# Hgrn mixer of a two-block denoiser on one core: heads in pieces inside projection blocks, and the output product taken apart by heads

## The reference, cut to what matters

```python
def hgrn2_mixer(h_lat, h_ctx, w_in, ...):            # 512 latent and 256 context tokens
    qc, vc, zfc, zbc, gc = _hgrn_inputs(h_ctx, w_in)    # h @ w_in, 1024 x 5120, in 8 heads of 128
    ql, vl, zfl, zbl, gl = _hgrn_inputs(h_lat, w_in)
    ... _gate(z, lb): log_f = log(lb + (1-lb) sigmoid(z)), k = (1-lb) sigmoid(-z), both directions
    ... _gla_scan in chunks of 64 tokens, forward and backward:
        cum = cumsum(log_f); scores = (q exp(cum-ref)) (k exp(ref-cum))^T, masked by a triangle
        S_next = exp(last) S + k^T v; o = scores v + (q exp(cum)) S
    y_lat = _hgrn_readout(o_lf + _rev(o_lb), gl, gnorm, w_out)

def _hgrn_readout(o, g, gnorm, w_out):
    o = o * rsqrt(mean(o * o, -1) + EPS) * gnorm        # per head
    y = o * silu(g)
    return y @ w_out                                     # 1024 x 1024, the sum goes over all 8 heads

x_lat = x_lat + g1 * y_lat
```

## Time and profile before

| | us |
|---|---|
| median of three runs (lowest, highest) | 3496.42 (3491.14, 3500.28) |
| the profiled execution | 3493.21 |
| its span | 3491.5 |
| mean granted TensorE clock | 0.947 |
| TensorE busy (products) | 3158.1, 90% |
| VectorE busy | 1861.7, 53% |
| ScalarE busy | 1387.5, 40% |
| the mixer with its output product, from the first block to the norm sum behind it | about 90 to 736 us of the span |

### The profile page before, as it was taken

One profiled execution on the slowest core, in us unless ns is written; L12 is line 12 of the kernel. 1 busy time (PEld: TensorE's weight loads), 2 busy tenths in 40 slices (PEclk: granted clock), 3 DMA queues, 4 the chain that ended last, 5 costly groups with the idle time before them and its releaser, 6 DMA issues.

```text
span 3491.5 us, 44906 instructions
## 1 busy us (share of the span) xinstructions
PE 3158.1 (90%) x16582; PEld 2570.7 (74%) x16582; DVE 1861.7 (53%) x2627; ACT 1387.5 (40%) x1905; POOL 116.1 (3%) x121
## 2 busy tenths in 40 slices
PE   5988888578996999899888999999998999889997
PEld 4777777467875888766776888878887778678886
DVE  6554555367985443678536534563446333454435
ACT  4445544446874222456314322342224332342222
POOL 0000000000000000043100000000000000000000
PEclk8999989698998999999998999999999999999998
DMA  4311211138992222221001222222222222123322
GB/s 170 127 55 57 70 54 54 37 120 337 390 359 83 96 96 96 85 71 61 23 2 61 96 96 96 102 88 97 93 95 97 73 73 90 50 71 103 101 97 73
DMA packets 98049, 357.66 MB, mean 102 GB/s; under 512 B 11008, under 2 KB 11392, under 8 KB 97536
## 3 DMA queue, kind: packets, MB, share of 16 engines
q1 hardware_dynamic: 92448, 334.54, 27.5%
q0 software_dynamic: 4176, 15.24, 1.2%
q10 hardware_dynamic: 1296, 6.11, 0.5%
HBM read 344.29 MB, written 11.56 MB: 102 GB/s over the span
## 4 chain that ended last, share of the span: by engine, by line
PE 78%; DVE 9%; ACT 7%; issue 4%; DMA 1%; POOL 0%; ACTq 0%; DVEq 0%; POOLq 0%
PE bank L281 20%; PE bank L282 19%; PE bank L283 19%; PE bank L1622 1%; PE bank L1624 1%; PE bank L1623 1%; PE gbank L920 1%; ACT whi L259 1%; PE bank L2603 1%; ACT L352 1%; DVE cum L1066 1%; PE gbank L902 1%; PE gbank L937 1%; PE bank L1651 1%; PE bank L1650 1%
## 5 line engine op out<-in xcount | busy, mean ns | idle before, releaser
L281 PE MATMUL bank<-h_hi_buf,whi 128*128 128x512 f32 x2320 | 929.5, 401 | 53.7 <-DVE h_lo_buf L450 33.9
L282 PE MATMUL bank<-h_lo_buf,whi 128*128 128x512 f32 x2320 | 912.6, 393 | 0.0
L283 PE MATMUL bank<-h_hi_buf,wlo 128*128 128x512 f32 x2320 | 911.0, 393 | 0.0
L259 ACT ACTIVATE whi<-raw 128x1024 fp32r<-128x1024 f32 x466 | 477.3, 1049 | 456.5 <-PE bank L283 402.3
L272 DVE TENSOR_TENSOR wlo<-raw,whi 128x1024 fp32r<-128x1024 f32 x444 | 533.4, 1221 | 138.6 <-ACT whi L259 71.8
L281 PEld LDWEIGHTS bank<-h_hi_buf,whi 128*128 128x128 f32 x2320 | 442.4, 191 | 167.5 <-DVE h_lo_buf L450 42.7
L282 PEld LDWEIGHTS bank<-h_lo_buf,whi 128*128 128x128 f32 x2320 | 442.2, 191 | 95.2 <-issue 5.3
L283 PEld LDWEIGHTS bank<-h_hi_buf,wlo 128*128 128x128 f32 x2320 | 441.4, 190 | 93.9
L281 PE MATMUL bank<-a_hi_buf,whi 128*128 128x512 f32 x960 | 377.1, 393 | 25.0 <-DVE a_lo_buf L3184 9.6
L282 PE MATMUL bank<-a_lo_buf,whi 128*128 128x512 f32 x960 | 375.7, 391 | 0.0
L283 PE MATMUL bank<-a_hi_buf,wlo 128*128 128x512 f32 x960 | 375.6, 391 | 0.0
(11 more groups left out here) (512 smaller groups left out, 3803.3 us busy)
## 6 DMA issues: line engine op xcount, KB each, us to landing
raw<-in_w SPq DMA_DIRECT2D x634, 512.0 KB, 3.4
x<-in_x ACTq DMA_DIRECT2D x2, 2048.0 KB, 10.8
sorted_rows<-zrow POOLq DMA_DIRECT2D x7, 514.0 KB, 8.4
xrow<-sorted_rows POOLq DMA_DIRECT2D x7, 514.0 KB, 7.5
sorted_y<-ysb POOLq DMA_DIRECT2D x7, 512.0 KB, 7.4
out<-x SPq DMA_DIRECT2D x8, 256.0 KB, 2.0
xc<-in_xc ACTq DMA_DIRECT2D x1, 1024.0 KB, 8.7
waup<-in_waup ACTq DMA_DIRECT2D x1, 256.0 KB, 5.2
```

The costliest lines, as they stand in the source:

```text
L259: act.activation(k.whi[:, g.slot, :], k.raw[:, g.slot, :], ACT.Copy).then_inc(k.split_hi, 1)
L281: pe.matmul(out, w_hi, hi, start=(t == 0), stop=False)
L282: pe.matmul(out, w_hi, lo, start=False, stop=False)
L283: return pe.matmul(out, w_lo, hi, start=False, stop=(t == tiles - 1))
```

## The change

**Three stages of the pipeline in place of two.** In iteration h the blocks of head h are multiplied, head e = h - 1 goes through its mixer, and the readout of head f = h - 2 is finished (squares, norm, gate, high and low part of y). Iterations 0 to 2 are unrolled, 3 to 7 are the loop.

**TensorE's pieces lie inside blocks.** `pe_block` already takes a call per tile (`ready`); it is now used to issue the pieces between the tiles of a block: the norm sum of f in block 0 at tile 4, v's transposes behind block 0, the two keys' in QB at tiles 4 and 7, the scores and the first state lot in VB at tiles 2 and 6, the second and third state lot in GB at tiles 0 and 4, the output behind GB.

**State products over 64 rows.** The products take rows 0 to 63 or 64 to 127 of `ktok` and of the one full `vtok`; `v_half` is gone with its four copies and its memset. The lots are three in place of six, and hold both directions; the bank goes by the half of rows (`c % 2`), no longer by the direction.

**The output product by heads.** A tile is (o, t): output rows o, head t. `PARTIAL` lists the 56 tiles of the first seven heads; the weights are packed in that order on the host (`partial_blocks`), the eight tiles of the last head in a block of their own. `pe_tail` multiplies the 56 (`fill(n)` takes the next n tiles of the list) between the pieces of head 7's mixer, into the four banks and `cbank`. VectorE adds each finished partial sum into x (`dve_partial`, eight times); `HgrnOutput` then multiplies the last head's eight tiles and VectorE adds these too. x is asked for when the last projection block is done. The memset of `ssq` is gone.

```diff
+EARLY = [(o, t) for o in range(RING + 1) for t in range(HEADS - 2)]
+PARTIAL = EARLY + [(o, HEADS - 2) for o in range(RING + 1)] + [(o, t) for o in range(RING + 1, DC) for t in range(HEADS - 1)]
+
+
+def partial_bank(k, o):
+
+    return k.bank[o] if o < RING else k.cbank if o == RING else k.bank[o - RING - 1]
...
+        def at_first(t):
...
+            if f is not None and t == 4:
+                self.pe_norm(k, q, f)
+
+        def at_query(t):
+            if e is not None and t in (4, 7):
+                self.pe_keys(k, e, 0 if t == 4 else 1)
+
+        def at_value(t):
+            if e is not None and t == 2:
+                self.pe_scores(k, e)
+            if e is not None and t == 6:
+                self.pe_states(k, e, 0)
+
+        def at_gate(t):
+            if e is not None and t in (0, 4):
+                self.pe_states(k, e, 1 if t == 0 else 2)
...
+        pe_block(k, g + ZB, DC, lat, more=(con, h.count(3, 1)))
+        pe_block(k, g + QB, DC, lat, ready=at_query)
+        pe_block(k, g + VB, DC, lat, more=(con, h.count(3, 2)), ready=at_value)
+        pe_block(k, g + GB, DC, lat, ready=at_gate)
         if e is not None:
+            self.pe_output(k, e)
...
+        for i, j in enumerate(range(4 * lot, min(4 * lot + 4, STEPS))):
+            for d in range(2):
                 c = CHAIN[d][j]
+                half = slice(CH * (c % 2), CH * (c % 2) + CH)
+                last = pe.matmul(k.gbank[c % 2][:, i * P:(i + 1) * P], k.ktok[half, d, c // 2, :], k.vtok[half, c // 2, :],
+                                 start=True, stop=True)
+        last.then_inc(k.gla_full, 1)
...
+    def pe_tail(self, k, q, e, f):
+
...
+        fill(4)
+        self.pe_norm(k, q, f)
+        self.pe_values(k, e)
+        fill(len(EARLY) - 4)
+        for d in range(2):
+            self.pe_keys(k, e, d)
+        fill(2)
+        self.pe_scores(k, e)
+        fill(3)
+        for lot, behind in enumerate((3, 4, 4)):
+            self.pe_states(k, e, lot)
+            fill(behind)
+        self.pe_output(k, e)
+        fill(4)
+        self.pe_norm(k, q, e)
+        fill(len(PARTIAL) - n)
+
+    def pe_partial(self, k, g, n):
+
         pe = k.nc.tensor
+        o, t = PARTIAL[n]
+        b = n // DC
+        out = partial_bank(k, o)[:, :]
+        wait(pe, k.split_lo, g + b + 1)
+        wait(pe, k.y_parts, t + 1)
+        if t == 0 and o < RING:
+            wait(pe, k.bank_free, g)
+        elif t == 0:
+            wait(pe, k.cbank_free if o == RING else k.partial_taken, 3 * HEADS if o == RING else o - RING)
+        w = slice(n % DC * P, (n % DC + 1) * P)
+        w_hi, w_lo = k.whi[:, (g + b) % RING, w], k.wlo[:, (g + b) % RING, w]
+        pe.matmul(out, w_hi, k.a_hi_buf[:, t, :], start=(t == 0), stop=False)
+        pe.matmul(out, w_hi, k.a_lo_buf[:, t, :], start=False, stop=False)
+        last = pe.matmul(out, w_lo, k.a_hi_buf[:, t, :], start=False, stop=(t == HEADS - 2))
+        if n % DC == DC - 1:
+            last.then_inc(k.block_done, 1)
+        elif t == HEADS - 2:
+            last.then_inc(k.out_full, 1)
...
+    def act_iteration(self, k, q, h, e, f):
+        g = h.n.times(HEAD_BLOCKS) + q.g
         def split(b):
+            act_split(k, g + b + LEAD)
         split(0)
+        if f is not None:
+            self.act_square_of(k, f)
         split(1)
         if e is not None:
+            self.act_sigmoids(k, q, e, f)
         split(2)
         if e is not None:
+            self.act_decays(k, e)
+        if f is not None:
+            self.act_norm_log(k, q, f)
         if e is not None:
+            self.act_turned(k, e, 0, k.vtok)
         split(3)
+        if f is not None:
+            self.act_norm_exp(k, q, f)
         if e is not None:
+            self.act_exponents(k, e)
         split(4)
         split(5)
         split(6)
         if e is not None:
+            self.act_turned(k, e, 2, k.ktok[:, 0])
+        if f is not None:
+            self.act_high(k, f)
+        if e is not None:
+            self.act_turned(k, e, 4, k.ktok[:, 1])
         split(7)
         if e is not None:
+            self.act_states(k, e, range(3, STEPS))
...
+        g = q.g + self.blocks
+        act.wait_ge(k.block_done, g)
+        act.dma_start(k.x[:, :, :], k.xT).then_inc(k.x_loaded, 16)
+        self.act_square_of(k, f)
+        self.act_sigmoids(k, q, e, f)
+        act_split(k, At(g + LEAD))
+        self.act_decays(k, e)
+        self.act_norm_log(k, q, f)
+        self.act_turned(k, e, 0, k.vtok)
+        act_split(k, At(g + LEAD + 1))
+        self.act_norm_exp(k, q, f)
+        self.act_exponents(k, e)
+        act_split(k, At(g + LEAD + 2))
+        self.act_high(k, f)
+        self.act_turned(k, e, 2, k.ktok[:, 0])
+        self.act_turned(k, e, 4, k.ktok[:, 1])
+        act_split(k, At(g + LEAD + 3))
+        self.act_states(k, e, range(3, 7))
+        act_split(k, At(g + LEAD + 4))
+        self.act_states(k, e, range(7, STEPS))
+        self.act_square_of(k, e)
+        act_split(k, At(g + LEAD + 5))
+        self.act_norm_log(k, q, e)
+        self.act_norm_exp(k, q, e)
+        self.act_high(k, e)
...
+        split(0)
+        if f is not None:
+            self.dve_gated(k, f)
+        split(1)
         if e is not None:
         take(0, k.z_st[:, 0, :], context=True)
+        if e is not None:
+            self.dve_silus(k, e)
         split(2)
         if e is not None:
+            for d in range(2):
+                self.dve_scan(k, e, d)
+        wait(dve, k.block_done, g + MOD_BLOCKS + 1)
+        dve_mod(k, k.bank[1][:, 0:MOD_BLOCKS * P], MOD_BLOCKS, h.n.times(MOD_BLOCKS) + 2 * DC, 0,
+                h.n + 2 * (2 * DC // RING), g + MOD_BLOCKS + 1, MOD_BLOCKS)
         split(3)
         if e is not None:
+            self.dve_keys(k, e)
         take(ZB, k.z_st[:, 1, :], context=True)
         split(4)
+        if f is not None:
+            self.dve_scaled(k, q, f)
         split(5)
         if e is not None:
+            wait(dve, k.qq_done, e.count(2, 2))
+        take(QB, k.q_st[:, :])
+        split(6)
+        if f is not None:
+            self.dve_low(k, f, e)
+        if e is not None:
+            if f is None:
+                wait(dve, k.gla_full, e.count(G_HEAD, N_TOK + N_SC))
             for d in range(2):
                 dve.copy_predicated(k.pt[:, d, :, :], k.pt_mask[:, d, :, :],
                                     k.gbank[d][:, :].rearrange("p (j t) -> p j t", t=P)).then_inc(k.pt_ready, 1)
+            self.dve_chain(k, e, 0)
         take(VB, k.v_st[:, :], context=True)
         if e is not None:
+            self.dve_chain(k, e, 1)
+            self.dve_chain(k, e, 2)
             wait(dve, k.silg_done, e.count(1, 1))
         take(GB, k.g_st[:, :])
         split(7)
         if e is not None:
+            self.dve_taken(k, e)
...
+        g = q.g + self.blocks
+        self.dve_gated(k, f)
+        self.dve_residual_gates(k)
+        self.dve_silus(k, e)
+        dve_split(k, At(g + LEAD))
+        for d in range(2):
+            self.dve_scan(k, e, d)
+        dve_split(k, At(g + LEAD + 1))
+        self.dve_keys(k, e)
+        wait(dve, k.qq_done, e.count(2, 2))
+        self.dve_scaled(k, q, f)
+        dve_split(k, At(g + LEAD + 2))
+        self.dve_low(k, f)
+        dve.wait_ge(k.x_loaded, 48)
+        for o in range(2):
+            self.dve_partial(k, g, o)
+        self.dve_masked(k, e)
+        self.dve_chain(k, e, 0)
+        self.dve_partial(k, g, 2)
+        self.dve_chain(k, e, 1)
+        dve_split(k, At(g + LEAD + 3))
+        self.dve_chain(k, e, 2)
+        for o in range(3, RING + 1):
+            self.dve_partial(k, g, o)
+        dve_split(k, At(g + LEAD + 4))
+        self.dve_taken(k, e)
+        self.dve_partial(k, g, RING + 1)
+        self.dve_gated(k, e)
+        self.dve_partial(k, g, RING + 2)
+        self.dve_scaled(k, q, e)
+        self.dve_low(k, e)
+        dve_split(k, At(g + LEAD + 5))
...
         pe = k.nc.tensor
+        t = HEADS - 1
+        wait(pe, k.split_lo, q.g + DC)
         pe.wait_ge(k.y_parts, HEADS)
+        for o in range(DC):
+            if o < RING:
+                wait(pe, k.partial_taken, o + RING + 2 if o < RING - 1 else RING)
+            else:
+                wait(pe, k.bank_free, q.g + o - RING + 1)
+            out, slot, w = k.bank[o % RING][:, :], (q.g + DC - 1) % RING, slice(o * P, (o + 1) * P)
+            pe.matmul(out, k.whi[:, slot, w], k.a_hi_buf[:, t, :], start=True, stop=False)
+            pe.matmul(out, k.whi[:, slot, w], k.a_lo_buf[:, t, :], start=False, stop=False)
+            last = pe.matmul(out, k.wlo[:, slot, w], k.a_hi_buf[:, t, :], start=False, stop=True)
+            last.then_inc(k.out_full if o < DC - 1 else k.block_done, 1)
 
     def act(self, k, q):
         act = k.nc.scalar
         k.sq, k.h32 = k.sq0, k.h320
+        for c in range(DC):
+            act_square(k, k.x[:, c, :], At(c + q.sq), lambda act: wait(act, k.bank_free, q.g + c + 1))
```

(16 more changed lines are left out.)

479 lines of the change are left out of this document (241 added, 238 removed).

## The result

The changed kernel takes **3343.3 us** (median of 4 runs, 3340.4 to 3345.7) against 3493.8 for the kernel before beside it (4 runs, 3488.2 to 3500.3): 0.9568 of its time, 95% interval 0.9549 to 0.9588. The profiled execution took 3340.36 us, its span is 3338.6.

A forecast was written before the change was run, and what follows sets the result against it. TensorE, with 78% of the critical chain, was taken as the bound, idling inside mixer lumps. Gains 86.4 (six periods), 6 (first) and 41.5 (last head), 134 us, took 3493.2 to 3359; plus 3.2 for the median, 3362; range 3344 to 3392.

The forecast's parts named there:

- The period without the state products: Loop head on TensorE: 54.9 us of full-clock work in all, counting 22 state products at 0.225 each.
- The 64-row products: State products in the loop: still 22 and not overlapping, with 0.2 us a lot for switching, 0.6 a head.
- the overlap rival: State products: consecutive ones in opposite row halves run together, saving 2.5 us a head, 3344; chance 0.05.
- Waits and hand-overs left in the loop: TensorE in a loop head: waits of 9.5 us shrink to about 0.5, plus 0.3 for hand-overs.
- The walk: Loop head followed engine by engine from the preceding output; tightest at the q block, its split 0.4 us ahead.
- "waits move" rival: Q block and state chain in the loop miss by 1 to 2 us each per head: 3385; chance 0.22.
- The half clock: TensorE in the loop: about 4 us a head lost at 1.2 GHz, forecast to go, granted clock 0.99 or more.
- The rival that it stays: Small pieces still let TensorE's clock fall: 4 us a head and 2 in the tail remain, 3392; chance 0.10.
- The last head: From head 6's output to the norm sum: 115.5 us becomes 74, gain 41.5, with 56 tiles multiplied meanwhile.
- "+5 on the path": Last head: added splits, head 6's norm and scaling, and partial sums on ScalarE and VectorE lengthen the path about 5 us.
- Nothing behind it changes: Mixture-of-experts stage behind the mixer: moves earlier as a whole, its weight rings starting from TensorE's progress.
- the overlap case: State products in opposite row halves running together, 2.5 us off each head, setting the low end 3344; chance 0.05.

The follow-up runs named there:

- the first experiment: Changed kernel with the state products of a lot reordered, rows 0 to 63 first, then rows 64 to 127: 3352.8 us, ratio 0.9602.
- the late-split runs: Changed kernel with VectorE's q-block weight split moved behind the keys: 3377.3 us; or between the two directions' keys: 3351.8 us.
- the last experiment: Changed kernel with two VectorE splits ahead of the last head's masked scores and scaling, the two last behind the last chunk's square: 3336.0 us, ratio 0.9545.

## Why the forecast was right in kind and short in size

Step by step, as the prediction put them:

- **The period without the state products**: 54.9 less 4.95, 49.9, is right. The measured period is 53.7; the lots take 1.09 + 1.09 + 0.87 and three times 0.2 of drain, 3.6. That leaves 50.1.
- **The 64-row products: the step that failed.** The sum had 4.95 and 0.6 of drain, 5.55; measured 3.6. The drain around a lot was right to 0.01. The error is in reading. "By the row they do not: eight records of the attention's, also in alternate halves, in 0.86 us, 0.108 each" took the eight records for products of 128 columns, as the row's shape says. But a row of the timeline that joins neighbours shows the shape of one. Kept apart by shape, the trace of before has in that window (1514.7 to 1515.58):

```profile
L2121 PE MATMUL bank<-kv_a,q_a 64*128 64x256 f32 x4 | 0.6, 377 | 0.0
L2121 PE MATMUL bank<-kv_a,q_a 64*128 64x128 f32 x4 | 0.5, 322 | 0.0
```

  Two records of 128 columns take 0.225 us, two of 512 take 0.85 (1.12 less the tail), so cost goes with the columns; four of 256 and four of 128 would be 0.85 + 0.45 = 1.3 one after the other. As pairs they are half of that, 0.65, and 0.2 for the two ends, 0.85; they took 0.86. The row that the prediction set against the overlap rival was evidence for it. It was worth 1.9 us a head: 22 products in 22 x 0.111 + 3 x 0.2, the measured 1.09 + 1.09 + 0.87 = 3.05, instead of 4.95. Sorting the halves in the first experiment takes 1.5 of it away and not all, since three pairs of records remain in each lot.
- **Waits and hand-overs left in the loop** (0.5 + 0.3): measured none. The walk itself stands: the q block's split was forecast 21.6 behind the output against a need at 22.0, and is ready at 21.9 (262.49) against 22.1 (262.69), counted from 240.56. The "waits move" rival (0.22) fell with this, and the late-split runs show what it would have been, 8.5 us for one of 1.3 a head. Products and waits together, 1.9 + 0.8 less the 0.2 more in the rest, are the 2.5 a head, 15.3 in six periods, by which the loop beats the forecast, and most of the 3.9 in the first.
- **The half clock**: forecast gone, and gone (1.00 in every loop head); in head 7 3.4 us of it are left, behind the wait of 1.8. The rival that it stays (0.10) fell.
- **The last head**: right in size, 73.3 for 74, in part by luck. Low half at 58.5 (forecast 58), last split at 59.6 (59), then 13.7 of sums and squares. The prediction priced these at 12.8, which gives 71.8; its 74 has 2.2 us more, for which it names no term, and 0.9 of them were there. Two splits in the 12.8 need not be there, as the last experiment shows. What the walk had not seen is that up to the taking TensorE is the bound: the "+5 on the path" of VectorE and ScalarE was in truth TensorE's own work, with one wait of 1.8 and the half clock behind it. So the low half at 58 was met by another path than the forecast's.
- **Nothing behind it changes**: -0.8 of 2755, right.
- **Range and odds**: the low end, 3344, was the overlap case, which had 0.05. It came true, and the 0.7 us between it and the measurement are luck: that case took 2.5 us off each head for two products running together. The overlap was worth 1.9, since the ends of a lot cost 0.2 inside it, and the waits that vanished made up the rest. The two cases were not put together, so a range whose ends are single cases was too narrow.

## What to carry to other kernels

Work that waits for a chain on other engines is hidden by putting independent tiles between its pieces, not by making the pieces faster: the faster products in the old order gave 12 us, the same products in the right order are part of 150. Look then for the narrowest slack in that order (here 0.2 us at one weight split) and keep it, since a delay there comes back in every pass, and a wait of 2.8 us cost 1.6 more at half clock. A half clock costs something only where TensorE sets the pace (here nothing at a period of 58.5 that the splits set). Before a row that joins several instructions is used as a price, ask for it by shape.
